# Partition swaps as DMA copies, 64-row score products and a 64-column compression operand in a two-block sequence model on one Trainium2 core

## The reference, cut to what matters

```python
def apply_rope(t, cos, sin):
    t1, t2 = jnp.split(t, 2, axis=-1)
    return jnp.concatenate([t1 * c - t2 * s, t1 * s + t2 * c], axis=-1)
```

```python
logits = jnp.einsum('bqgrd,bkgd->bgrqk', qb, kb) * scale + bias
```

```python
idx = jnp.arange(n_cmp)[:, None] * CMP_STRIDE + jnp.arange(CMP_BLOCK)[None, :]
blocks = kv[:, idx] + pos[None, None, :, None, :]
return jax.nn.gelu(blocks @ w1) @ w2
```

## Time and profile before

| | |
|---|---|
| median of 3 runs | 895.31 us (894.59 to 895.65) |
| the profiled execution | 896.43 us |
| its span, first to last instruction | 894.30 us |
| PE busy | 875.1 us, 98% |
| PE weight load busy | 779.4 us, 87% |
| DVE busy | 644.5 us, 72% |
| ACT busy | 437.5 us, 49% |
| POOL busy | 44.5 us, 5% |
| 1 MB weight loads of `w_in` (both blocks), median to landing | 6.6 us |

### The profile page before, as it was taken

How to read it: one execution, slowest core, us unless ns; L and a number is a source line. 1 busy time by engine, 2 the same in 40 slices (tenths; PEclk the granted TensorE clock), 3 DMA queues, 4 the chain that set the end, 5 groups by cost and what they waited for, 6 DMA issues and landing times.

```text
span 894.3 us, 14177 instructions
## 1 busy us (share of the span) xinstructions
PE 875.1 (98%) x5555; PEld 779.4 (87%) x5559; DVE 644.5 (72%) x806; ACT 437.5 (49%) x551; POOL 44.5 (5%) x50
## 2 busy tenths in 40 slices
PE   8999999999999999999999999999999999999995
PEld 5888888888998888888888999898998999999994
DVE  5685765767667676776776867666776888778776
ACT  6444444445334454444544545557434565555552
POOL 1100000002141000000001001200000000000000
PEclk9999999999999999999999999999999999999998
DMA  8866565545533468576466554434745446555531
GB/s 260 281 216 206 172 202 189 178 155 175 188 128 119 141 212 273 181 227 212 146 196 173 138 147 102 146 102 117 253 142 188 142 165 211 182 193 188 168 136 47
DMA packets 118303, 156.42 MB, mean 175 GB/s; under 512 B 4188, under 2 KB 104076, under 8 KB 118140
## 3 DMA queue, kind: packets, MB, share of 16 engines
q1 hardware_dynamic: 115964, 150.19, 53.0%
q0 software_dynamic: 1200, 4.68, 1.5%
q10 hardware_dynamic: 1104, 1.05, 0.4%
HBM read 154.84 MB, written 1.07 MB: 174 GB/s over the span
## 4 chain that ended last, share of the span: by engine, by line
PE 84%; DVE 9%; ACT 3%; DMA 2%; issue 1%; SPq 0%; DVEq 0%; ACTq 0%
PE wk L1443 29%; PE acc L1553 22%; PE wk L1468 16%; PE wk L1466 8%; DVE w_lo L839 3%; PE wk L1803 1%; DMA raw<-in_ffn_w 1%; PE acc L1775 1%; ACT w_hi L428 1%; ACT w_hi L435 1%; PE acc L1788 1%; DVE w_lo L845 1%; DMA raw<-in_w_in 1%; DVE xhl L850 1%; DVE work L1387 1%
## 5 line engine op out<-in xcount | busy, mean ns | idle before, releaser
L1443 PE MATMUL wk<-xhl,w_hi 128*128 128x256 f32 x1472 | 272.7, 287 | 1.6 <-DVE arena L1041 1.3
L1468 PE MATMUL wk<-xhl,w_hi 128*128 128x512 f32 x704 | 250.8, 399 | 0.0
L845 DVE TENSOR_TENSOR w_lo<-raw,w_hi 128x2048 fp32r<-128x2048 f32 x83 | 190.0, 2289 | 80.3 <-ACT w_hi L435 79.8
L1443 PEld LDWEIGHTS wk<-xhl,w_hi 128*128 128x128 f32 x1472 | 230.3, 192 | 6.1 <-issue 4.4
L1443 PE MATMUL wk<-xhl,w_lo 128*128 128x256 f32 x736 | 208.1, 283 | 0.0
L1466 PE MATMUL wk<-xhl,w_lo 128*128 128x256 f32 x704 | 199.3, 283 | 1.8 <-issue 0.8
L435 ACT ACTIVATE w_hi<-raw 128x2048 fp32r<-128x2048 f32 x83 | 157.9, 1904 | 26.7 <-PE wk L1443 26.6
L1468 PEld LDWEIGHTS wk<-xhl,w_hi 128*128 128x128 f32 x704 | 133.0, 189 | 32.1
L1553 PE MATMUL acc<-w_hi,hhl 128*128 128x512 f32 x480 | 153.6, 391 | 1.1 <-DVE w_lo L845 1.1
L839 DVE TENSOR_TENSOR w_lo<-raw,w_hi 128x2048 fp32r<-128x2048 f32 x56 | 129.4, 2314 | 24.3 <-ACT w_hi L428 24.2
L1443 PEld LDWEIGHTS wk<-xhl,w_lo 128*128 128x128 f32 x736 | 140.9, 191 | 0.0
(11 more groups left out here) (250 smaller groups left out, 919.8 us busy)
## 6 DMA issues: line engine op xcount, KB each, us to landing
raw<-in_ffn_w SPq DMA_DIRECT2D x65, 1024.0 KB, 5.4
raw<-in_w_in SPq DMA_DIRECT2D x26, 1024.0 KB, 6.6
raw<-in_w_ffn_in SPq DMA_DIRECT2D x22, 1024.0 KB, 5.1
raw<-in_w_ffn_out SPq DMA_DIRECT2D x11, 1024.0 KB, 4.8
raw<-in_w_out SPq DMA_DIRECT2D x8, 1024.0 KB, 4.8
arena<-bias_scratch POOLq DMA_DIRECT2D x4, 512.0 KB, 6.0
raw<-in_cmp_w_k SPq DMA_DIRECT2D x2, 1024.0 KB, 5.3
raw<-in_cmp_w_v SPq DMA_DIRECT2D x2, 1024.0 KB, 5.6
```

Source lines behind the costliest of these rows:

```text
L845: nc.vector.tensor_tensor(w_lo[:, s], raw[:, s], w_hi[:, s].bitcast(F32), ALU.subtract) \
L1443: mm = nc.tensor.matmul(dst, w, v, start=start and n == 0, stop=stop and n == len(pairs) - 1, skip_group_check=True)
L1468: return nc.tensor.matmul(bank, wh[:, c, cols], xhl[:, c].rearrange("p n t -> p (n t)"), start=False, stop=c == DC - 1, skip_group_check=True)
```

## The change

It has four parts.

1. First block: the four `swap_halves` products go. SP issues two DMAs for each (partitions 0 to 63 to 64 to 127 and back, SBUF to SBUF, 128 KB each) into a new tile `turned_s`. They stand in SP's program behind the loads of units `U_MIX` + 5 to 8, each with a wait for `proj_out`. `rope` reads SBUF instead of PSUM.
2. Second block: the permutation products of `swap_keys` and the one in unit 6 go. For each attention SP issues two DMAs of 64 KB from `kf` into `kz`; those of the first attention stand in front of the load of unit 8, those of the second in front of unit 13, those of the third in front of unit 14. The compressed ones (two DMAs of 128 KB) stand in front of unit 11. PE waits for the first DMAs (`key_in`) at slots 0, 6 and 12. POOL no longer clears `kz`, and ACT makes one copy where it made three.
3. The scores: each 512-column product over 128 rows becomes two of 256 columns over 64 rows (for tokens 0 to 127: four of 128 columns), the upper half of the rows into bank 1 of `acc`, the lower into bank 0. Both banks now belong to one slot, so PE waits before each slot for the previous one to be read (`logit_out` of s instead of s - 1). DVE reads the scores of the slots with four heads in two instructions instead of one.
4. Compression: high and low parts of the blocks are one stationary operand of 64 columns, so three passes become two (64 + 32 columns), with 64 rows of output; the transposes in unit 18 multiply by `fold`, which also adds the two halves.

```diff
+            def swap_rows(dst, src, done):
+
+                for lo_row in (0, HD):
+                    sp.dma_start(dst[lo_row:lo_row + HD], src[HD - lo_row:P - lo_row]).then_inc(done, 16)
+
             for m, c in enumerate((2, 3, 4, 5, 0, 1, 6, 7, 8, 9)):
                 unit(U_MIX + m, w_in[:, :, c * UC:(c + 1) * UC], DC)
+                if 5 <= m < 9:
+                    j = m - 5
+                    sp.wait_ge(proj_out, j + 1)
+                    swap_rows(turned_s[:, j], (q_s, k_s)[j // 2][:, 2 * (j % 2):2 * (j % 2) + 2], swapped[j])
...
+            def swap_keys(n, n_out):
+
+                sp.wait_ge(proj2, n_out)
+                if n == 2:
+                    sp.wait_ge(score_mm, 6)
+                for g in range(2):
+                    dst, src = slice(HD * (1 - g), HD * (2 - g)), slice(HD * g, HD * (g + 1))
+                    sp.dma_start(kz[n % 2][dst, g], kf[src, n]).then_inc(key_in[n], 16)
+
             for m in range(20):
+                if m == 8:
+                    swap_keys(0, 3)
+                if m == 11:
+                    sp.wait_ge(proj2, 6)
+                    swap_rows(cmp_turned, kf[:, K_CK:K_CV + 1], cmp_in)
+                if m == 13:
+                    swap_keys(1, 7)
+                if m == 14:
+                    swap_keys(2, 8)
...
-                act.wait_ge(key_swapped, (1, 3, 4)[n])
-                act.wait_ge(kz_zero, 2)
+                act.wait_ge(value_turned, n + 1)
...
-                nc.scalar.activation(z[0:HD, 1, 0], bank[0:HD, 0:T], ACT.Copy)
-                nc.scalar.activation(z[HD:P, 0, 1], bank[HD:P, 0:T], ACT.Copy).then_inc(kz_ready, 1)
+                bank = acc[:, (0, 0, 1)[n]]
+                nc.scalar.activation(v2[n % 2], k_n(bank[:, T:2 * T], 2), ACT.Copy).then_inc(kz_ready, 1)
...
-                dve.wait_ge(swapped, j + 1)
+                dve.wait_ge(swapped[j], 16 * 2)
...
-                step(nc.vector.tensor_tensor(tmp, halves(acc[:, j]), table_bc(T_SIN, 2), ALU.mult))
+                step(nc.vector.tensor_tensor(tmp, turned_s[:, j], table_bc(T_SIN, 2), ALU.mult))
...
+                        for j in range(nh // 2):
+                            done = nc.vector.scalar_tensor_tensor(
+                                out=lg[:, 2 * j:2 * j + 2], in0=acc[:, 0:2, j * n:(j + 1) * n], scalar=HD ** -0.5,
+                                in1=bias[:, hb + 2 * j:hb + 2 * j + 2, 0:n][:, :, ::-1], op0=ALU.mult, op1=ALU.add)
...
-                            src = kf[rows, K_CK + v] if g == s else acc[rows, 0, v * T:(v + 1) * T]
+                            src = kf[rows, K_CK + v] if g == s else cmp_turned[rows, v]
...
-            def swap_halves(j):
-                src, h = (q_s, k_s)[j // 2], 2 * (j % 2)
-                pe.wait_ge(proj_out, 1 + j)
-                nc.tensor.matmul(acc[:, j], swap, src[:, h:h + 2], start=True, stop=True).then_inc(swapped, 1)
...
+                            pe.wait_ge(key_in[r], 16 * 2)
                             pe.wait_ge(kz_direct, 2 * r + 2)
-                        if s >= 2:
-                            pe.wait_ge(logit_out, s - 1)
...
+                        if s:
+                            pe.wait_ge(logit_out, s)
+                        tiles, n, toks = ((w,), T, slice(P, T)) if w < 4 else ((2 * w - 8, 2 * w - 7), P, slice(0, P))
+                        for j in tiles:
+                            for side in range(2):
+                                cols = slice((j - tiles[0]) * n, (j - tiles[0] + 1) * n)
+                                rows = slice(HD * side, HD * (side + 1))
+                                mm = nc.tensor.matmul(acc[:, side, cols], q[rows, j, toks], z[rows, j // 2, 0:n],
+                                                      start=True, stop=True)
...
-                            bh, bl = (t[:, v, j0 + j] for t in blk_hl)
-                            mm = passes(wk[0:32, 0, v * T:(v + 1) * T],
-                                        ((bh, wh[:, j]), (bl, wh[:, j]), (bh, wl[:, j])), False, j0 + j == 15)
+                            last = j0 + j == 15
+                            nc.tensor.matmul(wk[0:32, 0, v * T:(v + 1) * T], blk_hl[0][:, v, j0 + j], wl[:, j],
+                                             start=False, stop=False, skip_group_check=True)
+                            mm = nc.tensor.matmul(wk[0:64, 0, v * T:(v + 1) * T], blk_wide[:, v, j0 + j], wh[:, j],
+                                                  start=False, stop=last, skip_group_check=True)
...
-                    if at == (6, 1):
-                        pe.wait_ge(proj2, 6)
-                        pe.wait_ge(logit_out, 5)
-                        nc.tensor.matmul(acc[:, 0], swap, kf[:, K_CK:K_CV + 1], start=True, stop=True) \
-                            .then_inc(key_swapped, 1)
```

More of the change, by code:

```diff
@@ L203, in build @@
         blk = carve(24, 2, 16, 32)
-        kz = [carve(32 + 4 * n, 2, 2, T) for n in range(2)]
+        kz = [carve(32 + 4 * n, 2, T) for n in range(2)]
         qa_s, qb_s = carve(40, 4, T), carve(44, 4, T)
@@ L210, in build @@
         v_blk = carve(48, 8, HD)
-        hid_rows = carve(50, 512)[0:32]
+        hid_rows = carve(50, 512)[0:64]
+        cmp_turned = carve(34, 2, T)
         prob_ct = carve(52, 2, P)
@@ L271, in build @@
         proj_out = sem("proj_out")
-        swapped, rope_cos, rope_out = sem("swapped"), sem("rope_cos"), sem("rope_out")
+        swapped = [sem(f"swapped{j}") for j in range(4)]
+        rope_cos, rope_out = sem("rope_cos"), sem("rope_out")
+        key_in = [sem(f"key_in{n}") for n in range(3)]
+        cmp_in = sem("cmp_in")
         pool_win, pooled_out, pool_mm, pool_hi, pool_lo = (
@@ L286, in build @@
                              "gate_taken"))
-        proj2, key_swapped, kz_zero, kz_direct, kz_ready = (
-            sem(n) for n in ("proj2", "key_swapped", "kz_zero", "kz_direct", "kz_ready"))
+        proj2, value_turned, kz_zero, kz_direct, kz_ready = (
+            sem(n) for n in ("proj2", "value_turned", "kz_zero", "kz_direct", "kz_ready"))
         ga_tanh = sem("ga_tanh")
@@ L786, in _ @@
             pool.wait_ge(head_lo, 2)
-            for z in kz:
-                nc.gpsimd.memset(z, 0.0).then_inc(kz_zero, 1)
             nc.gpsimd.memset(blk, 0.0).then_inc(blk_zero, 1)
@@ L820, in _ @@
             pool.wait_ge(kz_direct, 6)
+            for n in range(3):
+                pool.wait_ge(key_in[n], 16 * 2)
+            pool.wait_ge(cmp_in, 16 * 2)
             for c0, name in ((0, "cmp_w2_k_2"), (HD, "cmp_w2_k_2"), (2 * HD, "cmp_w2_v_2")):
@@ L1766, in attend @@
                     r, w = divmod(s, 6)
-                    q, z, bank = (qa_s if r == 0 else qb_s), kz[r % 2], acc[:, s % 2]
+                    q, z = (qa_s if r == 0 else qb_s), kz[r % 2]
                     if slot_time(s) == k:
@@ L1770, in attend @@
                             pe.wait_ge(kz_ready, 3 if r else 1)
+                            pe.wait_ge(key_in[r], 16 * 2)
                             pe.wait_ge(kz_direct, 2 * r + 2)
-                        if s >= 2:
-                            pe.wait_ge(logit_out, s - 1)
-                        if w < 4:
-                            mm = nc.tensor.matmul(bank, q[:, w, P:T], z[:, w // 2], start=True, stop=True)
-                        else:
-                            for j in (2 * w - 8, 2 * w - 7):
-                                mm = nc.tensor.matmul(bank[:, (j % 2) * T:(j % 2 + 1) * T], q[:, j, 0:P],
-                                                      z[:, w - 4, :, 0:P], start=True, stop=True)
+                        if s:
[7 more added lines that the diff above has]
+                                                      start=True, stop=True)
                         mm.then_inc(score_mm, 1)
@@ L1806, in attend, with turn_values @@
                         mm.then_inc(pv_mm, 1)
-            def swap_keys(n, bank):
-                nc.tensor.matmul(bank[:, 0:T], swap, kf[:, n], start=True, stop=True)
+            def turn_values(n, bank):
                 for tt in range(2):
@@ L1895, in _ @@
                         for n in range(4):
-                            mm = nc.tensor.transpose(wk[:, 0, 32 * n:32 * (n + 1)], hid_rows[:, n * P:(n + 1) * P],
-                                                     ident[0:32, 0:32])
+                            mm = nc.tensor.matmul(wk[:, 0, 32 * n:32 * (n + 1)], hid_rows[:, n * P:(n + 1) * P], fold,
+                                                  start=True, stop=True)
                         mm.then_inc(hid_turned, 1)
@@ L1970, in constants @@
     small[:, C_ID:C_ID + P] = np.eye(P)
-    small[:, C_SWAP:C_SWAP + P] = np.roll(np.eye(P), 64, axis=0)
+    small[:, C_FOLD:C_FOLD + 32] = (np.arange(P)[:, None] % 32) == np.arange(32)[None]
     q = np.arange(P)[:, None, None] + P * np.arange(2)[None, :, None]
```

39 lines of the change are left out of this document (15 added, 24 removed).

## The result

The changed kernel takes 903.8 us, median of 9 runs (900.3 to 908.2). The kernel before beside it takes 895.65 (894.6 to 897.7). The ratio is 1.0098, 95% interval 1.0078 to 1.0117: 8.2 us slower by the medians. The prediction said 897.7, slower by 2.4, with a range up to 902.0.

What follows compares the result with a forecast made beforehand. PE was taken as the bound, holding 84% of the chain of waits. Terms -3.44 + 1.6 + 3.6 + 1.7 - 0.7 - 0.4 = +2.4 on 895.31 gave 897.7 us, range 891.0 to 902.0.

Steps and rivals of the forecast that it cites:

- swaps of the first block: First block: four permutation products of 0.86 us leave PE's chain, the copies landing in time: -3.44 us.
- keys of the first attention: Slot 0: key copies queue behind unit 7's load, PE waits 2.0 us, slot starts later: +1.6 us.
- keys of the second attention: Slot 6: key copies stand behind unit 12's load, PE waits 5.3 us, slot starts later: +3.6 us.
- clock behind slot 6: After PE's 5.3 us wait at slot 6 the clock is down; getting back costs +1.7 us, bounds 0 to 3.
- scores: 18 score slots: partial overlap saves 0.11 in two-head slots, four-head slots lose 0.10; sum -0.7 us.
- compression ahead of slot 17: Only one half unit's saving lies before the last scores: -0.47, plus 0.1 for DVE's second instruction; -0.4 us.
- whole-overlap: Score products: rival that upper and lower rows run fully side by side, -6.0 instead of -0.7: 892.4 us; chance 0.18.
- no-overlap: Score products: rival that the row halves do not overlap at all, +1.8 instead of -0.7: 900.2 us; chance 0.25.
- Mode changes between outputs of 32 and 64 rows: Compression: rival that each such change costs PE 0.1 us over 64 products, together +1.6: 899.3 us; chance 0.08.
- the case named for it: Range's lower end, 891.0 us: score row halves fully side by side, with a load of 7.5 us at slot 6.

Runs made afterwards that it cites:

- part 4 alone: Kernel before with only the compression edit (64-column operand, fold product instead of transposes): 897.53 us, +2.4 us against before.
- early_fold: Changed kernel with key copies ahead of the loads of units 7, 12, 13 and DVE copying hidden rows ahead of unit 19's low part: 888.06 us.
- three_pass_fold: early_fold with the compression edit undone (three passes of 32 rows, transposes instead of the fold product): 888.99 us, -6.8 us against the kernel before.
- early_fold_y: early_fold with DVE's low parts of units 16 and 17 moved ahead of scaling the third attention's output: 887.18 us, -8.1 us against the kernel before.
- part 1 alone: Kernel before with only the first block's four permutation products made copies in SP's queue: 892.03 us, -3.8 us against before.

## Why the prediction was right in direction and wrong in size

The sum was +2.4; the profiled executions show +9.3, the medians +8.2. Of the 6.9 us between sum and profile, 4.1 are the clock, 2.7 the late keys and 0.6 the fold; the scores and the rest take 0.5 back. By its own steps:

| step | predicted | shown |
|---|---|---|
| swaps of the first block | -3.44 | -3.38 |
| keys of the first attention | +1.6 | +3.2 |
| clock behind slot 0 | none | +1.5 |
| keys of the second attention | +3.6 | +4.7 |
| clock behind slot 6 | +1.7 | +2.8 |
| scores (14 of the 18 slots; the others are in the rows around) | -0.7 for all | -1.3 |
| compression ahead of slot 17 | -0.4 | -0.5 |
| fold (0.64) and clock behind it (1.48) | none | +2.1 |
| rest (slot 17 to fold) | 0 | +0.2 |

- **Swaps: right** in size. The rotation never waited for a copy, but the cover was thinner than forecast: the first pair landed at about 220.4, 1.0 us and not 2.1 before DVE wanted it at 221.43. I gave no price to the rotation's product that now reads SBUF instead of PSUM; three of the four take 1.78 us instead of 0.68, and this lay beside PE's work.
- **Keys, both attentions: mechanism right in what it does, the size off by 2.7 us.** The rule "the copies are there 0.4 us after the load ahead of them" held within 0.2 us: the load of unit 7, issued at 506.65, took 8.7 and landed at 515.35, the copies at 515.95; that of unit 12 took 8.9 from 556.27, 565.2, the copies at 565.72. I took 7.5 and 7.9 for the two loads, each from one row, while other rows in the same place showed 9.5. Another 0.25 and 0.35 us pass from landing to the first product, which I had not counted. The reason I gave, an order inside SP's queue, is not needed, by the run with GpSimd's queue: a load under way is enough.
- **The clock: the step that failed.** I expected it to fall once, after the longer wait, and gave 1.7 us. It fell three times and cost about 5.8 us (1.5 + 2.8 + 1.5, the last being the 2.12 less 0.64 for the fold). Slot 0, with a forecast wait of 2.0 us, and the wait ahead of the fold had no term for the clock, and I gave no reason for leaving them out; the waits were 3.45 and 1.81 us. The price at slot 6 was within my bounds of 0 to 3. In the run with products of zeros the clock did not fall at slots 0 and 6.
- **Scores: right for the slots of two heads** (0.65 + 0.10 forecast for products and change; 0.63 and 0.15 in the chain), wrong for those of four heads, to which I gave no overlap: 0.65 with eight instructions. The whole-overlap and the no-overlap rivals both fall. Of the two sentences of the Trainium skill (TensorE: Matmul & The Clock Gate, "The mechanism") that I weighed, the first alone doesn't fit the trace and both together do: with both instructions of a side in program order, about three quarters of the time remain (0.63 of 0.86 us) and not half.
- **Compression: right that the saved products only lengthen waits, wrong that this is free.** I wrote that seven of the eight savings "only lengthen these waits", of which the one at the fold was 0.49 us. It became 1.81 us in the changed kernel and 2.94 us in part 4 alone, and a longer wait of PE has a price of its own, the clock. That PE's eight fold instructions cost 0.64 more than four transposes I had not priced at all, though the diff shows the edit.
- **Mode changes between outputs of 32 and 64 rows: nothing.** In the timeline of PE of the changed kernel such products follow each other every 0.11 to 0.12 us, the same as all of 32 rows. The rule of the Trainium skill (TensorEngine Tiling (Array Packing), "Key Properties"), that a change of mode drains TensorE, does not show between these outputs. Between products over 64 and over 128 rows something is lost, 0.15 us in the transposes behind the scores and 0.21 instead of 0.12 us from the last weight product to the scores; that this is the drain is not shown.

```profile
618.94 0.28 PE L1874 MATMUL wk<-w_lo,mhl 128*32 128x256 f32 x1
619.05 0.28 PE L1876 MATMUL wk<-w_hi,mhl 128*64 128x256 f32 x1
```

The range ended at 902.0 because each bound was taken by itself: the load of 9.5 at slot 6 stood with one fall of the clock, never with three. Its lower end does not follow from the case named for it either: 892.4 with a load of 7.5 instead of 7.9 gives 892.0, not 891.0.

The changed kernel's runs also spread over 8 us, those of before over 3. Each of its two waits ends with the landing of a 1 MB load, and such landings varied by 1 to 2 us between runs. The slower runs also have the lower mean granted clock: 0.993 at 900.3 us, 0.984 and 0.986 at the two of 908. A longer wait lowers this mean by itself, so it doesn't separate the landings from the clock; that these two make the whole spread is only argued.

## What to carry to other kernels

Where PE is the bound, price a wait of PE as the wait plus what the clock takes behind it. Where it fell this was 1.5 to 3 us here; it fell behind every wait for late copies and behind seven of the eleven waits ahead of the fold. Look for such waits also where the change only makes PE's own work shorter. A small copy on whose landing the bound engine depends belongs ahead of a large load, not behind it; another engine's queue doesn't replace that. And read the price of a product over one whole period of the loop, with the products behind it, not at the product alone.

## What the runs showed of the hardware that I had not expected

- A copy of 64 KB within SBUF landed in 2.5 to 3.6 us when it was issued about 5 us after a 1 MB load, and in 5.2 to 8.8 us when 0.4 to 2.2 us after one; on GpSimd's queue it was 5.2 to 7.4 us.
- Eleven profiled executions have a wait ahead of the fold. After waits of 0.43, 0.49, 1.65 and 1.72 us the 48 products took 5.94 or 5.95 us; after 1.65, 1.69, 1.81, 1.86, 2.25, 2.28 and 2.94 us they took 7.39 to 7.45; with no wait, in early_fold, three_pass_fold and early_fold_y, 5.95. Between 1.65 and 1.72 us it went either way. The kernel with part 1 alone, which changes nothing there, is among the slow ones in its profiled execution; its load of unit 19 took 7.98 us.
- The clock fell to 0.50 some 1.7 us after PE had taken up work again (slot 0), not only during the wait.
- A DVE product of 128 x 512 with both operands in SBUF took 1.78 us three times in the changed kernel, while GpSimd was at work on its own SBUF product, and 0.69 us the fourth time, with GpSimd idle. GpSimd's product took 3.27 us instead of 1.30. With one operand in PSUM, as before, DVE's took 0.68 though GpSimd was at work. Timelines of DVE and of GpSimd in the changed kernel:

```profile
226.77 1.79 DVE L1078 TENSOR_TENSOR work<-arena 128x512 f32<-128x512 f32 x1
...
224.74 3.27 POOL L799 TENSOR_TENSOR arena<-arena 128x512 f32<-128x512 f32 x1 [2.08 <-DVE arena L1070]
```
